# Moving the "high" and "low" passes of a stage's third weight unit around the norm at a stage boundary

## The reference

```
for l in range(DEPTH):                        # block 1, DEPTH = 2
    h = swiglu_ffn(rmsnorm(x, ffn1_pre_g[l]), ffn1_w_gu[l], ffn1_w_down[l])
    x = x + 0.5 * rmsnorm(h, ffn1_post_g[l])
    h = mixing_sublayer(rmsnorm(x, mix_pre_g[l]), w_in[l], ...)   # gMLP, pooling, sparse attention, convolution
    x = x + rmsnorm(h, mix_post_g[l])
    h = swiglu_ffn(rmsnorm(x, ffn2_pre_g[l]), ffn2_w_gu[l], ffn2_w_down[l])
    x = x + 0.5 * rmsnorm(h, ffn2_post_g[l])
for l in range(DEPTH):                        # block 2: shifts, scales and gates come from c
    n = _modulate(_rms_norm(h, norm_g[l, 0]), sh1, sc1)
    h = h + 0.5 * ga1 * _swiglu(n, ffn_w_in[l, 0], ffn_w_out[l, 0])
    ... # token mixing and a second swiglu in the same manner
return _rms_norm(h, final_norm_g)
```

## Time and profile before

| | |
|---|---|
| median of 3 runs | 2617.56 us |
| the profiled execution's own time | 2616.55 us |
| its span, first to last instruction | 2614.7 us |
| mean granted TensorE clock | 0.979 |
| PE busy | 2478.1 us (95%) |
| DVE busy | 1659.8 us (63%) |
| ACT busy | 1196.9 us (46%) |
| POOL busy | 290.0 us (11%) |

### The profile page before, as it was taken

The page is one execution under the profiler, slowest core; times in us unless marked ns, Lnnn a source line. Parts: engine busy times, 40 slices in busy tenths (PEclk is TensorE's granted clock), DMA queues, the critical chain, the costliest instruction groups (busy, mean ns, idle before and its releaser), DMA issues.

```text
span 2614.7 us, 34282 instructions
## 1 busy us (share of the span) xinstructions
PE 2478.1 (95%) x14089; PEld 2117.4 (81%) x14089; DVE 1659.8 (63%) x2099; ACT 1196.9 (46%) x1437; POOL 290.0 (11%) x384
## 2 busy tenths in 40 slices
PE   7999988999999998899999999989999999998998
PEld 5888987788788898778878888877887888887786
DVE  4775686677676668677677665556446446556544
ACT  4344454443433445344344335844434434693443
POOL 2000322000100041210010000110000000021000
PEclk9999999999999999999999999999999999999999
DMA  8784455687786444578668645445556555445553
GB/s 287 264 283 140 131 160 185 213 294 257 235 297 233 140 129 156 183 244 287 235 229 302 234 139 143 133 153 186 197 174 203 183 171 148 136 130 169 194 182 108
DMA packets 369163, 514.27 MB, mean 197 GB/s; under 512 B 21600, under 2 KB 310614, under 8 KB 369008
## 3 DMA queue, kind: packets, MB, share of 16 engines
q1 hardware_dynamic: 342608, 415.80, 49.1%
q0 software_dynamic: 26400, 96.28, 10.4%
HBM read 510.89 MB, written 1.13 MB: 196 GB/s over the span
## 4 chain that ended last, share of the span: by engine, by line
PE 52%; DVE 5%; ACT 2%; issue 2%; POOL 0%; DVEq 0%; POOLq 0%; ACTq 0%
PE ps L1662 47%; DVE lo L1094 1%; PE ps L1708 1%; ACT hi L721 1%; PE ps L1848 1%; PE ps L1838 1%; PE ps L1857 0%; PE ps L1684 0%; PE ps L1810 0%; DVE arena L1153 0%; DVE arena L1159 0%; PE ps L2020 0%; PE ps L2003 0%; ACT arena L761 0%; ACT arena L853 0%
## 5 line engine op out<-in xcount | busy, mean ns | idle before, releaser
L1094 DVE TENSOR_TENSOR lo<-raw,hi 128x2048 fp32r<-128x2048 f32 (+1 forms) x400 | 922.4, 2307 | 605.1 <-ACT hi L721 604.5
L721 ACT ACTIVATE hi<-raw 128x2048 fp32r<-128x2048 f32 (+1 forms) x400 | 757.8, 1896 | 558.3 <-PE ps L1662 542.6
L1662 PE MATMUL ps<-hi,NH 128*128 128x512 f32 (+3 forms) x1760 | 682.9, 388 | 53.2 <-DVE NL L1587 28.2
L1662 PE MATMUL ps<-hi,NL 128*128 128x512 f32 (+3 forms) x1760 | 673.4, 383 | 0.0
L1662 PE MATMUL ps<-lo,NH 128*128 128x512 f32 (+3 forms) x1760 | 673.1, 382 | 0.0
L1662 PEld LDWEIGHTS ps<-hi,NH 128*128 128x128 f32 x1760 | 337.9, 192 | 127.4 <-DVE lo L1094 30.6
L1662 PE MATMUL ps<-NH,hi 128*128 128x256 f32 x1376 | 398.9, 290 | 15.8 <-DVE lo L1094 15.8
L1662 PE MATMUL ps<-NL,hi 128*128 128x256 f32 x1376 | 391.7, 285 | 0.0
L1662 PEld LDWEIGHTS ps<-hi,NL 128*128 128x128 f32 x1760 | 336.6, 191 | 67.4
L1662 PE MATMUL ps<-NH,lo 128*128 128x256 f32 x1376 | 390.5, 284 | 0.0
L1662 PEld LDWEIGHTS ps<-lo,NH 128*128 128x128 f32 x1760 | 337.5, 192 | 64.8
(11 more groups left out here) (300 smaller groups left out, 2123.8 us busy)
## 6 DMA issues: line engine op xcount, KB each, us to landing
raw<-in_ffn_w_gu SPq DMA_DIRECT2D x176, 512.0 KB, 4.8
raw<-in_ffn_w_in SPq DMA_DIRECT2D x176, 512.0 KB, 4.7
arena<-in_ada_w POOLq DMA_DIRECT2D x72, 1024.0 KB, 7.2
raw<-in_w_in SPq DMA_DIRECT2D x96, 512.0 KB, 4.5
raw<-in_ffn_w_down SPq DMA_DIRECT2D x88, 512.0 KB, 4.6
raw<-in_ffn_w_out SPq DMA_DIRECT2D x88, 512.0 KB, 4.1
raw<-in_mix_w_in SPq DMA_DIRECT2D x86, 512.0 KB, 4.5
raw<-in_w_branch SPq DMA_DIRECT2D x16, 512.0 KB, 4.1
```

The costliest lines, as they stand in the source:

```text
L721: last = nc.scalar.activation(dst, src, ACT.Copy)
L1094: last = nc.vector.tensor_tensor(dst, src, part.bitcast(F32), ALU.subtract)
L1662: last = nc.tensor.matmul(dst, a, b, start=start and k == 0, stop=stop and k == 2, skip_group_check=skip)
```

## The change

Three edits, none of which adds or removes an instruction.

1. ACT, feed-forward stages: `new_squares(p, 1)` is issued ahead of `split_hi(s, 2)`, no longer behind it.
2. ACT, mixing stages: `split_hi(s, 2)` is issued ahead of `normed(p, 1)`, no longer behind it.
3. DVE, mixing stages: `split_lo(s, 2)` is issued right behind `new_x(p, 1)`, ahead of `mean_square_new`, `norm` and `normed_rest`. In feed-forward stages DVE had it there already and is not touched.

```diff
@@ ACT, def ffn(s)
                 split_hi(s, 1)
                 out_squares(p, 1)
+                new_squares(p, 1)
                 split_hi(s, 2)
-                new_squares(p, 1)
                 m.stage = s.key
                 silu(s, 0, 0)
                 normed(p, 1)
@@ ACT, def mix(s)
                 split_hi(s, 1)
                 out_squares(p, 1)
                 new_squares(p, 1)
+                split_hi(s, 2)
                 normed(p, 1)
-                split_hi(s, 2)
                 m.stage = s.key
@@ DVE, def mix(s)
                 split_lo(s, 1)
                 new_x(p, 1)
+                split_lo(s, 2)
                 mean_square_new(p, 1)
                 norm(p, 1)
                 normed_rest(p, 1)
-                split_lo(s, 2)
                 m.stage = s.key
```

## The result

The changed kernel takes 2660.91 us (median of 4 runs, 2658.6 to 2661.44) against 2617.42 us (median of 4, 2616.55 to 2617.72): ratio 1.0163, 95% interval 1.015 to 1.0175, 43.5 us slower. The profiled execution took 2661.54 us, its span is 2659.7 us, the mean granted clock 0.967 where it was 0.979. It is the longest of the 21 executions of the changed kernel on record (2658.31 to 2661.54), and the one profiled before was the shortest of its four, so the two spans differ by 45.0 us where the medians differ by 43.5.

What follows compares the result with a forecast made beforehand. PE, busy 95% of the span, was taken as the bound, so only its idle time could win or lose. 2614.7 + 1.85 + 21.1 + 16.1 + 7 = 2660.8 us, forecast as 2660.5, range 2649 to 2670.

Steps and rivals of the forecast that it cites:

- Edit 1, 21.1 us: Seven feed-forward boundaries: the copy waits behind the squares, so PE resumes later, 5 x 3.1 + 2 x 2.8 us.
- The 0.3 us that `20f2` and `21f2` were to save at the turning: Block 2 feed-forward stages after mixing: `norm` no longer held 0.3 us by the gate product, so delay 2.8, not 3.1.
- second stops: Block 2 feed-forward stages: PE's four further stops before the turning, 1.1 us of each taken as filled, 4.5 in all.
- Edits 2 and 3, 16.1 us: Four mixing boundaries: `lo` waits for the copy and delays `mean_square_new`, 4 x 4.0 us; PE's gap goes to 8.3.
- a rise of about 16 us for all waits for `norm`: Sign to look for: PE's summed wait for `norm` rises by about 16 us.
- The clock, 7 us net: Longer PE gaps at eleven boundaries lower the clock behind them: 10.5 plus 1 less 4.5 us; bounds 0 and 22.
- The five stages whose boundary had been at full clock: Feed-forward stages expected to get a new fall of the clock behind PE's gap: 2.1 us each, 10.5 in all.
- The delays are kept: Later mixing-stage work does not absorb the boundary delays, as DVE idles 9.49 and 1.66 us before its long stretch: 37.2 us.
- A: Rival: DVE's long stretch in mixing stages takes back their 16.1 us, giving 2644.7 us; chance 0.08.
- B: Rival: later waits in mixing stages absorb all but the last feed-forward stage's 2.8 us, giving 2619.4 us; chance 0.02.
- a shorter wait for `lo` deep in a mixing stage: Sign for A and B: PE's waits for `NL` or `lo` deep in the mixing stages shrink; no size given.
- `10f1` at nothing: First feed-forward stage: x is there from the start, `lo` of unit 2 ends about 0.7 us later, hidden, cost nothing.

Runs made afterwards that it cites:

- e1: Edit 1 alone (ACT's squares ahead of the copy of unit 2 in feed-forward stages) against the kernel before: 2645.88 us, ratio 1.0109.
- e3: Edit 2 alone (ACT's copy of unit 2 ahead of `normed` in mixing stages) against the kernel before: 2616.98 us, ratio 1.0001.
- e4: Kernel before with edit 3, and ACT's copy of unit 2 ahead of the squares in mixing stages: 2621.11 us, ratio 1.0016.
- e2: Edits 2 and 3 alone (mixing stages), feed-forward stages as in the kernel before: 2631.97 us, ratio 1.0056.
- e6: Kernel before with 50 matmuls of zeros ahead of the turning of tile 1 in the four mixing stages: 2610.59 us, ratio 0.9974.
- e8: Kernel before with matmuls of zeros in mixing gaps, feed-forward gaps and ahead of the output projection: 2603.43 us, ratio 0.9952.
- e5: Changed kernel with matmuls of zeros in eleven gaps, 65 in each of seven feed-forward stages, 110 in each of four mixing stages: 2651.05 us, ratio 1.0128.
- e7: Kernel before with unit 2's subtraction in feed-forward stages split into halves, the second between `mean_square_new` and `norm`: 2616.53 us, ratio 0.9993.
- e9: Kernel of e7 with the second half of the subtraction moved behind `norm`: 2613.26 us, ratio 0.9988 against the kernel before.

## Why the prediction was right, step by step

The forecast was 2660.5 us, the measurement 2660.91. The terms, each against the traces:

- **Edit 1, 21.1 us.** The waits for `lo` at the seven boundaries grew by 21.8 us. DVE's new idle time is 3.02 us where 3.1 was worked out; PE's gap is 5.48 where 5.5 was named, and 4.73 in `20f2` where 4.7 was. The 0.3 us that `20f2` and `21f2` were to save at the turning sit in the second stops, which are gone altogether. e1 shows that the term stands alone.
- **Edits 2 and 3, 16.1 us.** The gap in `10m` is 8.32 where 8.3 was named, and the four gaps grew by 16.1. e3 and e4 show the inner split: edit 2 nothing, edit 3 nearly all of it through the copy that it waits for. The prediction also named a rise of about 16 us for all waits for `norm`. That sum rose by 11.1 only, because the second stops, 5.0 us, are in it too; the prediction had taken them off the clock's term and forgot them in this sign.
- **The clock, 7 us net.** Measured: 13.0 us of busy time more, less the four second stops that PE no longer makes, 5.0 us: 8.0. The prediction had 11.5 less 4.5. The total is near, the parts are not all as forecast. The five stages whose boundary had been at full clock gained 8.7 us of busy time, 1.7 each, where 2.1 each, 10.5 in all, was taken. The other seven stages gained 4.4 where 1 was taken; half of it is in `10m`, well behind its boundary, where the prediction had nothing. That these two errors partly cancel is luck.
- **The delays are kept.** The waits for `NL` kept 28.2 us to the tenth, and in e1 and e2 they are 28.1: rivals A and B are out. What excluded them beforehand, DVE idle ahead of its long stretch, was enough. One sign that the prediction gave for A and B did appear, a shorter wait for `lo` deep in a mixing stage (3.83 to 2.19 us in `11m`). It hides some 1.6 us of the clock's cost, and the later wait in that stage ended by L1446 is 0.9 longer, so little of it is left; it does not touch the 16.1.
- **`10f1` at nothing.** The traces show it. After the change `lo` of unit 2 ends 0.6 us later there (26.50 for 25.89), the gate product starts 0.1 later (28.30 for 28.18), and PE turns tile 1 at 29.44 for 29.32.

Added up against the span: 21.8 and 16.1 us of waits, 8.0 for the clock, less 0.8 in the other waits, are the 45.0 but for rounding. The forecast had 44.2 from the same execution, so it is 0.8 us low there; that it meets the median of the changed kernel within 0.4 us is better than its terms deserve. The executions of that kernel spread over 3.2 us.

## What to carry to other kernels

Here, where each engine works through its list in order, an instruction moved behind one that waits for data inherits that wait, and so does whoever waits for it on another engine: before moving anything ask whether it fills a wait where it stands (here 1.9 us of copying inside 4.4 us of idle time, which became 3 us of DVE's and PE's). A consumer moved earlier wins nothing if its producer on the other engine can't be there in time, or if nobody was waiting for its result, and both were so for unit 2 in the mixing stages. A gap of TensorE can cost twice, once as idle time and once as the lower clock behind it. At the boundaries of the kernel before, the three gaps of 1.6 us were followed by full clock, of the four of 2.3 to 2.4 us two were and two were not, and all four of 4.3 us and more were followed by less. So matmuls of zeros placed in gaps that can't be closed are worth a try.

## What the runs showed of the hardware

**Small matmuls hold the clock.** Fifty matmuls of zeros (128x128, bf16) in each of four gaps of 4.3 to 4.7 us gave 7.4 us (e6), and with more of them in other gaps it was 12.6 us in all (e8). In e5 seven of the eleven filled gaps resumed at 1.00; unfilled, none of them did. Gap length alone does not decide: in e5 PE was idle for 1.83 us ahead of 481.4 and for 1.84 ahead of 687.7, and the clock behind them was 0.79 and 1.00.

**A root of one column can be held up by a subtraction.** POOL's inverse root took 1.46 or 1.47 us at the eight feed-forward starts of e7 and 0.55 or 0.56 at the same places of e9, since in e7 DVE subtracted 128x1024 values beside it. By the Trainium skill, page "SBUF — State Buffer", section "SBUF: two separate sides", an operation of VectorE with two SBUF inputs and one of GpSimd that reads SBUF take a shared pair of ports in turn, and the loser waits until the other is done. The trace agrees: the subtraction ends at 473.86 and the root at 474.26, 0.4 us behind it. The price falls on the small operation, and when that sits in a chain it is paid in full: `norm` started 3.0 us behind x's end in e7 and 2.0 in e9.
